# Mixture of experts: the first group gathered by a one-hot product, the router tile by tile, and three weight buffers in turn for home and spill units

## The reference, cut to what matters

```python
mix = concatenate([rec, att]) @ w_out          # 1024 x 1024
x = x + g1 * mix
h2 = _rms(x, norm2_g) * (1 + sc2) + sh2
g_logits = h2 @ w_rg + b_rg                    # 4 groups
g_top = argmax(g_logits); gate_g = softmax(g_logits)[g_top]
e_in = (h2 @ w_re + b_re).reshape(-1, 4, 4)[:, g_top]   # 4 experts of that group
top_v, top_j = top_k(e_in, 2)
w_sel = softmax(top_v) * gate_g
for e in range(16):                            # each token uses 2 of the 16
    y += combine[:, e] * ((silu(h2 @ w1[e]) * (h2 @ w3[e])) @ w2[e])
x = x + g2 * y
```

## Time and profile before

| | |
|---|---|
| median of three runs | 1724.33 us |
| profiled execution | 1731.76 us |
| its span, first to last instruction | 1730.0 us |
| PE busy | 1628.0 us, 94% of the span |
| DVE, ACT, POOL busy | 697.6, 256.3, 108.5 us |
| DMA, mean | 193 GB/s |

### The profile page before, as it was taken

One profiled execution on the slowest core, in us unless ns is written; L12 is line 12 of the kernel. 1 busy time (PEld: TensorE's weight loads), 2 busy tenths in 40 slices (PEclk: granted clock), 3 DMA queues, 4 the chain that ended last, 5 costly groups with the idle time before them and its releaser, 6 DMA issues.

```text
span 1730.0 us, 17356 instructions
## 1 busy us (share of the span) xinstructions
PE 1628.0 (94%) x6960; PEld 879.8 (51%) x6960; DVE 697.6 (40%) x1322; ACT 256.3 (15%) x576; POOL 108.5 (6%) x123
## 2 busy tenths in 40 slices
PE   4999999999999999999989999999989867999997
PEld 2445556474444444446655888448856533333332
DVE  1617853468886000112174765004584242111112
ACT  3121113010000000000053110000322311010110
POOL 1000001100000000001000000002030101100101
PEclk9999999999999999999989999999999978999999
DMA  9452441145666321107510799424623449999997
GB/s 338 169 195 99 145 173 47 50 157 206 227 210 222 118 97 49 48 1 281 200 49 1 257 332 360 147 97 158 195 96 122 146 158 356 390 390 391 392 388 263
DMA packets 160623, 333.94 MB, mean 193 GB/s; under 512 B 15288, under 2 KB 15568, under 8 KB 160544
## 3 DMA queue, kind: packets, MB, share of 16 engines
q1 hardware_dynamic: 141408, 298.90, 47.5%
q0 software_dynamic: 18224, 30.78, 5.4%
q10 hardware_dynamic: 912, 3.17, 0.5%
HBM read 355.02 MB, written 15.48 MB: 214 GB/s over the span
## 4 chain that ended last, share of the span: by engine, by line
PE 88%; DVE 4%; DMA 4%; issue 2%; POOL 1%; ACT 1%; SPq 0%; DVEq 0%; ACTq 0%; POOLq 0%
PE psum L624 84%; PE psum L628 4%; DMA wring<-in_ev_w_in 1%; DMA wring<-in_w_mod 1%; DMA wring<-in_mlp_w 1%; POOL small L1517 1%; ACT wide L1657 0%; DVE wide L2061 0%; DVE big L2394 0%; DMA x_slots<-wide,slot_i 0%; DVE big L2553 0%; DMA big<-x_slots 0%; DVE small L2552 0%; POOL x_slots L1603 0%; DVE small L2176 0%
## 5 line engine op out<-in xcount | busy, mean ns | idle before, releaser
L624 PE MATMUL psum<-wring,big 128*128 128x512 f32 (+2 forms) x1600 | 559.5, 579 | 12.4 <-issue 11.9
L624 PE MATMUL psum<-wide,wring 128*128 128x256 f32 (+3 forms) x1872 | 490.3, 437 | 0.3
L624 PEld LDWEIGHTS psum<-wring,big 128*128 128x128 f32 (+1 forms) x1600 | 243.0, 173 | 309.2 <-issue 305.2
L624 PEld LDWEIGHTS psum<-wide,wring 128*128 128x128 f32 (+1 forms) x1872 | 304.4, 184 | 173.0 <-issue 144.5
L624 PE MATMUL psum<-wring,wide 128*128 128x512 f32 (+3 forms) x576 | 216.0, 575 | 8.8 <-DMA wring<-in_w_mod 5.4
L1657 ACT ACTIVATE big<-psum 128x512 f32<-128x512 f32 (+2 forms) x155 | 83.1, 546 | 663.2 <-PE psum L624 614.3
L2061 DVE SCALAR_TENSOR_TENSOR wide<-wring,csilu,wide 128x512 f32<-128x512 f32 x252 | 175.5, 749 | 3.0
L624 PEld LDWEIGHTS psum<-wring,wide 128*128 128x128 f32 (+1 forms) x576 | 97.6, 188 | 109.1 <-issue 96.1
L2161 DVE TENSOR_TENSOR wide<-psum,gate 128x512 f32<-128x512 f32 x27 | 18.7, 691 | 333.1 <-PE psum L624 332.9
L1517 POOL TENSOR_TENSOR small<-small 128x1 f32<-128x1 f32 (+2 forms) x30 | 41.2, 1374 | 1045.6 <-DVE small L2178 884.5
L1657 ACT ACTIVATE wide<-psum 128x256 f32<-128x256 f32 (+2 forms) x114 | 46.1, 418 | 311.4 <-PE psum L628 157.3
(11 more groups left out here) (266 smaller groups left out, 892.5 us busy)
## 6 DMA issues: line engine op xcount, KB each, us to landing
wring<-in_mlp_w SPq DMA_DIRECT2D x32, 2048.0 KB, 8.8
wring<-in_w SPq DMA_DIRECT2D x32, 2048.0 KB, 21.5
wring<-in_w_mod SPq DMA_DIRECT2D x24, 2048.0 KB, 12.9
big<-in_w SPq DMA_DIRECT2D x23, 2048.0 KB, 20.1
wide<-in_w SPq DMA_DIRECT2D x14, 2048.0 KB
wring<-in_w_ada SPq DMA_DIRECT2D x12, 2048.0 KB, 8.7
wring<-in_w_in SPq DMA_DIRECT2D x8, 2048.0 KB, 8.6
wring<-in_ev_w_in SPq DMA_DIRECT2D x6, 2048.0 KB, 12.9
```

The lines of the kernel that those rows point to most:

```text
L624: return nc.tensor.matmul(o, a, b, start=first, stop=last)
```

## The change

- Order of units: 0, 1, 2, S0, 3, 4, S1, 5, 6, S2, 7, 8, S3, 9, 10, S4, 11, 12, S5, 13, S6, 14, 15.
- Buffers: three of w1/w3 and three of w2, used by position in the order modulo 3, home and spill alike. SP starts with load_up(0), load_down(0), load_up(2), load_down(1), load_down(2), load_up(1), and then load_up(i), load_down(i) for each i from 3. load_up(2) waits only for `yT211`.
- Router tile by tile: tile 2's rows are transposed between the last two halves of the projection, tile 3's after it; `xm` and `hTm` in `big` take the place of `xn` and `hT`, `yT2` and a scratch move to `lnb` and `big`. Each tile has its own logits bank, and the gate rows come after both.
- First group: DVE makes `first_hot`, 128 tokens x 128 slots for each of two token tiles, from the slot numbers; PE multiplies `xm` with it (16 products) into the banks that the eight transposes of group 0 filled. POOL still scatters all rows, but reads back from group 1 on.
- `turn_picks` stands after the first up, the wait for the kept picks at the third unit. On DVE the two route steps stand ahead of the position counts, and the modulation of group 0 ahead of the route weights and picks.

```diff
@@ moe_order
+    after = [2 * n + 2 for n in range(SPILLS - 1)] + [NEXP - LATE - 1]
-        if e % 2 == 1 and e // 2 < SPILLS:
-            order.append(NEXP + e // 2)
+        if e in after:
+            order.append(NEXP + after.index(e))
@@ buffers
-        yT2 = region(big, 0, KC, T)
+        yT2 = region(lnb[:, :, :].rearrange("p a b -> p (a b)"), 0, KC, T)
+        xm = region(big, 0, 2, D)
+        hTm = region(big, 2048, KC, T)
-        w2_spill = region(big, 4096, 4, D)
-        w2_ring = region(big, 8192, 2, 4, D)
+        w2_ring = region(big, 4096, 3, 4, D)
-        w13_spill = wide[:, 0:2 * KC * 512].rearrange("p (w k n) -> p w k n", w=2, k=KC)
+        w13_ring.append(wide[:, 0:2 * KC * 512].rearrange("p (w k n) -> p w k n", w=2, k=KC))
+        first_hot = region(lnb_flat, 0, 2, P)
+        first_slot = region(small, 112, 2, 2)
@@ TensorE
-            out_project(2, yT2, (2, 3))
-            pe.wait_ge(xn_ready, 4)
-            turn_x("moe", xn, (0, 1))
+            out_project(2, yT2, (2,))
+            out_project(2, yT2, (3,), lambda: turn_routed("moea", 0))
+            router("moea", 0)
+            turn_routed("moeb", 1)
+            router("moeb", 1)
             gate_rows(2, 1)
...
+            def gather_first():
+
+                pe.wait_ge(first_ready, 1)
+                for k in range(KC):
+                    for t in range(2):
+                        last = mm(psum[:, 4 + k // 4, (k % 4) * P:(k % 4 + 1) * P], xm[:, t, k * P:(k + 1) * P],
+                                  first_hot[:, t, :], t == 0, t == 1)
+                last.then_inc(xs_turned, 1)
@@ up, and down alike
-                if u < NEXP:
-                    w = w13_ring[u % 2]
-                    pe.wait_ge(w13_in[u % 2], 32 * (u // 2 + 1))
-                else:
-                    w = w13_spill
-                    pe.wait_ge(w13_in[2], 32 * (u - NEXP + 1))
+                w = w13_ring[i % 3]
+                pe.wait_ge(w13_in[i % 3], 32 * (i // 3 + 1))
@@ unit loop
-            turn_picks()
-            turn_group(GROUP_ORDER[0])
-            pe.wait_ge(late_ready, 1)
+            gather_first()
             for i in range(UNITS):
                 up(i)
+                if i == 0:
+                    turn_picks()
+                if i == 2:
+                    pe.wait_ge(late_ready, 1)
@@ SyncE
+            def load_up(i):
+
+                u = ORDER[i]
+                if i == 2:
+                    sp.wait_ge(bank_full, full("yT211"))
+                if i > 2:
+                    sp.wait_ge(up_done, i - 2)
...
+            def load_down(i):
+
+                u = ORDER[i]
+                if i < 3:
                     sp.wait_ge(bank_full, full("yT211"))
                 else:
-                    sp.wait_ge(down_done, AT[e - 2] + 1)
+                    sp.wait_ge(down_done, i - 2)
...
             load_up(0)
             load_down(0)
+            load_up(2)
+            load_down(1)
+            load_down(2)
             load_up(1)
...
+            for i in range(3, UNITS):
+                load_up(i)
+                load_down(i)
@@ GpSimd
-                                            in_=xn[:, t, :], in_offset=None).then_inc(x_spread, 16)
+                                            in_=xm[:, t, :], in_offset=None).then_inc(x_spread, 16)
...
-                if n > 1:
-                    pool.wait_ge(xs_turned, n - 1)
+                pool.wait_ge(xs_turned, max(n - 1, 1))
...
-            loaded = 0
+            loaded = 1
@@ VectorE
-                rms_row(t)
-            modulate("moe")
+                rms_row(t, xm)
+                modulate(("moea", "moeb")[t])
...
+            for t in range(2):
+                free(v_.tensor_tensor(lg[:, t, :], ready(f"router{t}")[:, 0:20], brr, ALU.add), f"router{t}")
...
             signal(v_.tensor_copy(slot_i[:, :], slot_f.rearrange("p c t -> p (c t)")), slots_ready)
+            step(v_.tensor_scalar(first_slot, slot_f, float((NEXP - LATE) * SLOTS), None, ALU.add))
+            for t in range(2):
+                step(v_.tensor_scalar(first_hot[:, t, :], cst("late"), first_slot[:, 0, t:t + 1], None, ALU.is_equal))
+            for t in range(2):
+                last = v_.scalar_tensor_tensor(first_hot[:, t, :], cst("late"), first_slot[:, 1, t:t + 1], first_hot[:, t, :],
+                                               ALU.is_equal, ALU.add)
+            last.then_inc(first_ready, 1)
```

More of the change, by code:

```diff
@@ L201, in build @@
     ORDER = moe_order()
-    AT = {u: i for i, u in enumerate(ORDER)}
     GROUP_OF = [u // 2 for u in ORDER]
@@ L1288, in _, with turn_routed, router @@
             gate_rows(2, 0)
-            out_project(2, yT2, (2, 3))
-            pe.wait_ge(xn_ready, 4)
-            turn_x("moe", xn, (0, 1))
-            gate_rows(2, 1)
-            wait_h("moe")
-            o = claim("router")
-            for t in range(2):
-                for k in range(KC):
-                    last = mm(o[:, t * 20:(t + 1) * 20], hT[:, k, t * P:(t + 1) * P], wr[:, k, :], k == 0, k == KC - 1)
-            last.then_inc(bank_full, 1)
+            def turn_routed(part, t):
+                pe.wait_ge(xn_ready, 3 + t)
+                turn_x(part, xm, (t,))
+            def router(part, t):
+                wait_h(part)
+                o = claim(f"router{t}")
+                for k in range(KC):
+                    last = mm(o[:, 0:20], hTm[:, k, t * P:(t + 1) * P], wr[:, k, :], k == 0, k == KC - 1)
+                last.then_inc(bank_full, 1)
+            out_project(2, yT2, (2,))
[3 more added lines that the diff above has]
+            router("moeb", 1)
+            gate_rows(2, 1)
             pe.wait_ge(ind_ready, 1)
@@ L1970, in _ @@
             gates(2, 0)
-            modulate("moe")
+            modulate("moea")
+            modulate("moeb")
             gates(2, 1)
@@ L2718, in _ @@
                     residual(2, "out2", half, (X0 + t,), alpha=1.0)
-                rms_row(t)
-            modulate("moe")
-            o = ready("router")
-            free(v_.tensor_tensor(lg, o[:, 0:40].rearrange("p (t e) -> p t e", t=2),
-                             brr.unsqueeze(1).to_broadcast([P, 2, 20]), ALU.add), "router")
-            dve.wait_ge(*moved("router"))
+                rms_row(t, xm)
[3 more added lines that the diff above has]
+            for t in range(2):
+                dve.wait_ge(*moved(f"router{t}"))
             pick = cst("pick")
@@ L2754, in _ @@
             signal(v_.tensor_tensor(ind, oh[:, 0], oh[:, 1], ALU.add), ind_ready)
+            rt_x4 = rt_exp.rearrange("p (t e) -> p t e", t=2)
+            step(v_.tensor_tensor(rt_x4[:, :, 0:4], lg[:, :, 0:4], each(rt_g), ALU.subtract))
+            signal(v_.tensor_tensor(rt_x4[:, :, 4], rt_2, rt_1, ALU.subtract), route_ready)
             o = ready("pos")
@@ L2786, in _, with modulate_group @@
             signal(v_.tensor_copy(table_i[:, :], table_f.rearrange("p a n -> p (a n)")), table_ready)
-            rt_x4 = rt_exp.rearrange("p (t e) -> p t e", t=2)
-            step(v_.tensor_tensor(rt_x4[:, :, 0:4], lg[:, :, 0:4], each(rt_g), ALU.subtract))
-            signal(v_.tensor_tensor(rt_x4[:, :, 4], rt_2, rt_1, ALU.subtract), route_ready)
+            def modulate_group(g):
+                dve.wait_ge(xs_turned, GROUP_AT[g] + 1)
+                for k in range(4, KC):
+                    last = v_.tensor_scalar(slots_of(g)[:, k, :], psum[:, 5, (k - 4) * P:(k - 3) * P], modc[:, 2, 32 + k, 0:1],
+                                            modc[:, 2, 24 + k, 0:1], ALU.mult, ALU.add)
+                last.then_inc(hs_ready, 1)
+            modulate_group(0)
             dve.wait_ge(route_exp, 1)
@@ L2811, in _ @@
             dve.sem_inc(pick_ready, 1)
-            def modulate_group(g):
-                dve.wait_ge(xs_turned, GROUP_AT[g] + 1)
-                for k in range(4, KC):
-                    last = v_.tensor_scalar(slots_of(g)[:, k, :], psum[:, 5, (k - 4) * P:(k - 3) * P], modc[:, 2, 32 + k, 0:1],
-                                            modc[:, 2, 24 + k, 0:1], ALU.mult, ALU.add)
-                last.then_inc(hs_ready, 1)
             def keep_y(i):
```

102 lines of the change are left out of this document (40 added, 62 removed).

## The result

The changed kernel takes 1739.68 us (median of 5 executions, 1734.50 to 1742.05) against 1724.33 us of the kernel before, measured beside it: a ratio of 1.0082, 95% interval 1.0059 to 1.0105. A second series gave 1.0031 (1.0008 to 1.0054, 12 executions). The change makes the kernel 0.3 to 0.8% slower; the forecast was 0.6% faster, and the range ended at 1722.

What follows compares the result with a forecast made beforehand. Products and weight stream were taken to nearly tie as the bound. The front gains 11.7 us, 11.5 us of waits stay by unit 17, and the last down ends 10.5 us sooner: 1713.8 us, range 1703 to 1722.

Steps and rivals of the forecast that it cites:

- What bounds the kernel now: Expert stage: TensorE's products and the weight stream nearly tie; stream taken at 381 GB/s, with 390 as the other end.
- Router, slot numbers, gather, picks: Ahead of the experts: router 3.0 us sooner, slots at 1420.4, gather records 5.8 us, first unit at 1429.7, picks +0.5.
- The stream of the first experts: SP's early loads, issued from 1368.6: all three first experts in by 1411, before the first unit starts.
- So 1436.7 + 1.6 + 194.8 = 1633.1: Weight stream to unit 17: start after the first up, 1.6 us idle, then 74.2 MB in 194.8 us at 381 GB/s.
- unit 17 (expert 12), the point that binds: Expert loop: stream arrives at 1633.1, TensorE without waits at 1621.6, so 11.5 us of waits by this unit, none later.
- priced it once (1.6 us): Start of the new weight stream: first w2 waits for a down to 1448.8, leaving the stream 1.6 us idle.
- For the first unit I had the price right, 1.6 us: First expert unit: starts at full clock, saving the 1.6 us that its half-clock start cost before.
- Rival 3: Expert loop: shared buffers starve, slower; decides from a load latency of about 26 us, priced there at 1732; chance 0.10.
- Rival 1: Expert loop: TensorE alone decides, three experts' lead covers every wait; gain 21.5 us, 1702.8 us; chance 0.14.
- rival 2: First unit hardly moves, or the stream starts later and eats the saving; 1717 to 1725 us; chance 0.14.
- Sum: Whole kernel: last down ends at 1707.5 instead of 1718.0, 10.5 us gained, median 1713.8 us.

Runs made afterwards that it cites:

- e13: e1 with each store of y as two transfers of 64 rows, still issued by GpSimd; 1711.12 us, 0.9896 of the kernel before.
- e16: The kernel before with only the two-piece stores of y (64 rows each); 1725.47 us, 0.9960 of the kernel before.
- e1: The changed kernel with SP issuing w1 and w3 of unit i+1 before w2 of unit i; 1722.56 us, 0.9966 of the kernel before.
- e11: The changed kernel with spare products fitted into the waits ahead of units 4, 5, 8, 11, 14, 17 and 22; 1732.44 us, 1.0014 of before.
- e15: The changed kernel, its order of loads kept, with only the two-piece stores of y; 1720.75 us, 0.9943 of the kernel before.
- e2: The changed kernel's router, gather and picks with the unit order, buffers and SP loads of before; 1725.05 us, 0.9972 of the kernel before.
- e7: e1 with each w2 load bringing only the first half of its rows; 1704.38 us, 0.9859 of the kernel before.
- e10: e1 without the 21 stores of y and the waits for them; 1705.12 us, 0.9872 of the kernel before.
- e4: e1 with the stores of y, each in one piece, issued from ScalarE instead of GpSimd; 1798.23 us, 1.0401 of the kernel before.
- e14: e1 with each store of y as two transfers of 64 rows, issued from ScalarE; 1713.18 us, 0.9910 of the kernel before.

## Why the prediction was wrong, step by step

**What bounds the kernel now: right, but read one layer short.** Products and stream do nearly tie: 265.9 us of TensorE alone against a stream whose shortage costs 10 us of waits. I worked with 381 GB/s and took the 390 at "full DMA share" as the upper end of what the engines give. They give 397 to 400 once the stores are even (e13), and 396 to 400 in the kernel before too (e16). The profile had a hint that I did not follow: the records of a load spread over 5.5 us.

**Router, slot numbers, gather, picks: right.** Forecast on the scale of before: router's add 1410.5, slots 1420.4, first up 1429.7. Measured, less 3.8: 1411.1, 1420.9, 1429.6. The router came 0.6 us late and the gather was 0.4 shorter than forecast, so the closeness of the last number is partly luck. The second router part did run at half clock (16 records in 3.57 us), the bound that I had allowed. The gather took 5.4 against 5.8. The table and the picks stayed under their cover (the picks ready 1.4 us before the first up's end). The stream of the first experts was in by 1413.5, with the 3.8 off 1409.7 against 1411.

**"So 1436.7 + 1.6 + 194.8 = 1633.1": this step failed.** "I work it out at unit 17 (expert 12), the point that binds." I divided all bytes up to one unit by one rate, and so had a stream that never thins. It does in every round of three units (365 to 385 GB/s in windows of 40 us, 327 in the last), because w1/w3 stand behind a w2 that waits for a down. What binds is each load by itself: 21 to 23 us of room from the issue to the need, 24 to 26 from the issue to the last engine. The places that this sum named were right (8, 11, 14, 17), and so nearly was their size (9.5 us against 11.5). Units 4, 5 and 22, 10.5 us more, were not in it, since no sum of bytes makes them late. I had written down the very order that does it, one paragraph above, and priced it once (1.6 us) instead of at each unit. e1, which swaps only that order, takes 11 to 14 us off the loop.

**The clock behind a wait: not priced at all.** 5.7 to 8.4 us at face value, some half of it by e11's profile. For the first unit I had the price right, 1.6 us; I did not carry it to the waits that I forecast myself.

**Unforeseen, and a second lever beside the order: the store's shape.** 5.7 to 8.4 us of loop on the changed kernel (e15), 6.3 on the one before (e16), 8.4 on e1 (e13).

**Rivals.** Rival 3 is what happened: shared buffers starve from a latency of about 26, and the waited loads had 24 to 26. Its chance of 0.10 was argued down with "the latency is mostly queue, and less is queued when less is issued". In the median that was so (19.6 us against 21.9); but the loads that were waited for go out in bursts, the w2 of one unit with the w1 and w3 of the next, and they took 24 to 26. Its price (1732 to 1740) holds the measured time as well. Its name was wrong, though: it is not the sharing (e1 beside e2) but the order. Rival 1's floor of 266 us is confirmed by e7 and e10, and rival 2 did not happen.

**Sum.** Forecast 10.5 us gained: front 10.1 + 1.6, loop otherwise about even. Measured between the two profiles: front 10.2 gained, loop 16.8 lost. The start of the first unit was right within 0.1 us. The loop was forecast at 277.8 us, and of the 17.2 us by which it was missed two terms make up 16.9: waits, 20.0 where 11.5 stood, and clock, 8.4 where none stood.

## What to carry to other kernels

When loads share one queue, don't price the stream by its bytes: write down for every load what stands ahead of it, when that can go, and the time from its issue to its last engine against the room until its use; a load that can go must not stand behind one that waits for a later event. Look at the shape of small transfers beside a full stream: stores whose outermost dimension is 2 cost this kernel's loop 6 to 8 us by unevenness, though they carry 5% of the bytes. And when you forecast waits of TensorE such as the 1.9 to 5.1 us here, ask whether the clock falls behind them: it did behind five of seven.

## What the runs showed of the hardware that I had not expected

- A store of 0.26 MB whose outermost dimension is 2, from ScalarE, left 3 completion records and drew the 16 engines of a load 11.7 us apart; the same bytes as two pieces of 64 rows 2.8 us. From GpSimd it was 5.5 against 2.3. The time: 1798 against 1713 us. Two of the sixteen engines are the late ones: in e4's w2 loads the last two report 6.5 to 16.8 us after the other fourteen.
- With even engines one core's full stream runs at 395 to 400 GB/s (e13, e14, e16), with uneven ones at 387 to 392 (before, e1); in its last window e13 has fallen to 377.
- The clock fell behind waits of 1.96 and 2.62 us and stayed up behind one of 3.10 in the same loop; in e15 also behind one of 3.16. The length of the wait alone does not tell it; what does, no run here settles.
- A spare product of 64 x 256 took 0.22 us a record, as long as one of 64 x 512. Why is open.
